# A convolution stage whose next tile is read out and gated between the last taps of the tile before it, with a ring of eight diagonals

## The chip, the cores and the metric

The kernel runs on one core of a Trainium2 chip. The metric is the device time of one execution in microseconds (us). Three executions of the kernel before took 2856.85, 2852.44 and 2855.83 us, median 2855.83. The engines are PE (TensorE; PEld is its weight load), DVE (VectorE), ACT (ScalarE), POOL (GpSimd) and SP (SyncE, which issues DMAs). Each works through its own instructions in the order in which they are written, and they meet only at semaphores.

## The reference

The kernel computes three blocks of a network with all its mixers and a mixture of experts. The change touches one stage of it, the convolution module of the second block, with D = 1024 channels and 512 tokens:

```python
CONV_C = 31
def causal_dwconv(x, w, b):           # one filter of 31 taps for each channel
    y = lax.conv_general_dilated(x, w[:, None, :], window_strides=(1,), padding=[(K - 1, 0)],
        dimension_numbers=("NWC", "WIO", "NWC"), feature_group_count=C)
    return y + b

def conformer_conv(x, norm, w1, b1, dw_w, dw_b, ln_g, ln_b, w2, b2):
    h = rms_norm(x, norm) @ w1 + b1   # 1024 -> 2048 channels
    h = jax.nn.glu(h, axis=-1)        # first half * sigmoid(second half)
    h = causal_dwconv(h, dw_w, dw_b)
    h = jax.nn.silu(layer_norm(h, ln_g, ln_b))
    return h @ w2 + b2
```

## The kernel before, in words

Channels lie on the 128 partitions and the 512 tokens along a row, so the stage has eight tiles j = 0 to 7 of 128 channels. Products in fp32 are made of three matmuls: each operand is split into a rounded high part and the remainder (hi·hi, hi·lo, lo·hi; `split_matmul`, line 526).

For tile j, in the words used below:

- **Projection** (PE, `pointwise` in `pe_conformer`): two banks, c1 (the value half) and c2 (the gate half), each 8 x 3 matmuls, 48 in all.
- **Read-out** (DVE, `pointwise` in `dve_conformer`): first the split of a unit of weights for a later tile (`w_lo`, line 513), then c2 times the norm's factor into `c_t2` (line 1560), then c1 into `c_t1` (line 1562).
- **Gating**: ACT takes the sigmoid of `c_t2` (line 1508), DVE makes `c_t1` = (c1 + bias) * sigmoid ("glu", line 1570, recorded at the helper's line 548).
- **Split of the gated tile**: ACT writes `c_t_hi` (line 1515), DVE the remainder `c_t_lo` (line 1580).
- **Taps on the vector side**: ACT starts `c_h` with the newest tap and the bias ("last tap", line 1511). DVE adds 17 more taps to it, one instruction each, each of which waits for the one before (lines 1573 to 1577, recorded at line 548; the width tells the tap: 495 columns is the first, 511 the last).
- **Taps on PE**: the 13 oldest taps are matmuls with a diagonal matrix of the tap's weights, 3 matmuls a tap, 39 a tile, into one bank. ACT makes each diagonal as two instructions, high and low (lines 1521, 1524), in a ring of 4 places: diagonal n waits until PE has used diagonal n - 4.
- **Joining** ("h", line 1587): DVE adds PE's bank to `c_h` when the tile's 13 diagonals are through.

PE runs one projection ahead: projection 0, projection 1, diagonals 0, projection 2, diagonals 1, and so on; at the end diagonals 6 and diagonals 7 follow one another. After them PE sums the eight tiles of `c_h` with a matrix of ones (16 matmul records), and the layer norm, which needs all eight tiles, begins with ACT's `c_mu` (line 1529). The orders on DVE and ACT are those of the Python loops; no scheduler changes them.

Of the kernel before, what the change touches and what calls it, by code (L numbers as in the profile page):

```python
# [8 lines left out]
F32 = mybir.dt.float32  # L9
# [7 lines left out]
P = 128  # L17
# [194 lines left out]
def build(nc, stream, vectors, consts, rconsts, x_in, mem_in, gates_w, group_w, lora_w,  # L212
# [95 lines left out]
    with ExitStack() as ph:  # L308
        c_s_hi, c_s_lo = sb(ph, "c_s_hi", [P, KT, S], F32R), sb(ph, "c_s_lo", [P, KT, S], F32R)
        c_h = sb(ph, "c_h", [P, KT, S])  # L310
        c_t1 = sb(ph, "c_t1", [P, 2, S])
        c_t2 = sb(ph, "c_t2", [P, 2, S])
        c_mu = sb(ph, "c_mu", [P, S])
        c_diag_hi, c_diag_lo = sb(ph, "c_diag_hi", [P, 4, P], F32R), sb(ph, "c_diag_lo", [P, 4, P], F32R)

        C_PAD = 16
        c_t_hi, c_t_lo = (sb(ph, f"c_t_{m}", [P, 2, C_PAD + S], F32R) for m in ("hi", "lo"))
        c_taps_hi, c_taps_lo = sb(ph, "c_taps_hi", [P, KT * CONV_C], F32R), sb(ph, "c_taps_lo", [P, KT * CONV_C])
# [209 lines left out]
    def split_matmul(T, out_ap, l_hi, l_lo, r_hi, r_lo, first, last):  # L528
        matmul(T, out_ap, l_hi, r_hi, first, False)
        matmul(T, out_ap, l_hi, r_lo, False, False)  # L530
        return matmul(T, out_ap, l_lo, r_hi, False, last)
# [925 lines left out]
    def pe_conformer(T):  # L1457
        n_diag = 0

        def pointwise(j):  # L1460
            n = place[("pw1", j)]
            b = take_bank(T, ("c1", j), dve_c, "t1", j)
            project(T, n, 2 * P, 0, ring1["xg"], range(KT), b, pe_c, ("c1", j), xg_ready(3) if j == 0 else None)
            b = take_bank(T, ("c2", j), dve_c, "t2", j)
            project(T, n, 2 * P, 1, ring1["xg"], range(KT), b, pe_c, ("c2", j))

        pointwise(0)
        for j in range(KT):
            i = j % 2
            if j + 1 < KT:  # L1470
                pointwise(j + 1)
            b = take_bank(T, ("conv", j), dve_c, "h", j)
            for m, k in enumerate(c_order):
                sh = CONV_C - 1 - k
                T.wait_ge(*act_c.at("diag", n_diag))
                if m == 0:
                    T.wait_ge(*dve_c.at("t_lo", j))
                odd = sh % 2
                moved = slice(C_PAD - odd, C_PAD + S - sh)
                split_matmul(T, b[:, sh - odd:], c_diag_hi[:, n_diag % 4, :], c_diag_lo[:, n_diag % 4, :],  # L1480
                             c_t_hi[:, i, moved], c_t_lo[:, i, moved], m == 0,
                             m == len(c_order) - 1).then_inc(*pe_c.mark("conv", n_diag))
                n_diag += 1
        b = take_bank(T, ("c_mean",), act_c, "mean")
        for j in range(KT):
            T.wait_ge(*dve_c.at("h", j))
            mm = matmul(T, b[:, :], const("ones"), c_h[:, j, :], j == 0, j == KT - 1)
        mm.then_inc(*pe_c.mark("mean"))
        b = take_bank(T, ("c_var",), act_c, "root")
        for j in range(KT):  # L1490
            T.wait_ge(*act_c.at("square", j))
            matmul(T, b[:, :], const("ones"), square[:, j % 2, :], j == 0, j == KT - 1).then_inc(*pe_c.mark("var", j))
        pe_out(T, units_of("pw2", 4), 2 * P, (c_s_hi, c_s_lo), range(KT), pe_c, ("x",), 4,
               ready=lambda k: dve_c.at("s_lo", k), after=lambda T: pe_xa_begin(T, 1))

    def act_conformer(A):
        n_diag = 0
        taps = slice(col["c_dw_w"], col["c_dw_w"] + KT * CONV_C)
        A.wait_ge(*normed(3))
        A.activation(c_taps_hi[:, :], vec[:, taps], ACT.Copy).then_inc(*act_c.mark("taps_hi"))  # L1500
        for part in (c_t_hi, c_t_lo):
            A.activation(part[:, :, 0:C_PAD], const("ident")[:, 0:2 * C_PAD].rearrange("p (i c) -> p i c", i=2),
                         ACT.Copy, scale=0.0).then_inc(*act_c.mark("zeros", part is c_t_lo))
        act_take(A, place[("pw1", 0)])
        for j in range(KT):
            i = j % 2
            A.wait_ge(*dve_c.at("t2", j))
            A.activation(c_t2[:, i, :], c_t2[:, i, :], ACT.Sigmoid, bias=vcol("c_b1", KT + j)).then_inc(
                *act_c.mark("sigmoid", j))
            A.wait_ge(*dve_c.at("glu", j))  # L1510
            A.activation(c_h[:, j, :], c_t1[:, i, :], ACT.Identity, scale=c_tap(j)(CONV_C - 1),  # L1511
                         bias=vcol("c_dw_b", j)).then_inc(*act_c.mark("last_tap", j))
            if j >= 2:
                A.wait_ge(*pe_c.at("conv", n_diag - len(c_order) - 1))
            A.activation(c_t_hi[:, i, C_PAD:], c_t1[:, i, :], ACT.Copy).then_inc(*act_c.mark("t_hi", j))
            if j + 1 < KT:
                act_take(A, place[("pw1", j + 1)])
            for k in c_order:
                if n_diag >= 4:
                    A.wait_ge(*pe_c.at("conv", n_diag - 4))  # L1520
                A.activation(c_diag_hi[:, n_diag % 4, :], const("ident"), ACT.Copy, scale=c_tap(j)(k)).then_inc(
                    *act_c.mark("diag_hi", n_diag))
                A.wait_ge(*dve_c.at("taps_lo"))
                A.activation(c_diag_lo[:, n_diag % 4, :], const("ident"), ACT.Copy,
                             scale=c_taps_lo[:, CONV_C * j + k:CONV_C * j + k + 1]).then_inc(
                    *act_c.mark("diag", n_diag))
                n_diag += 1
        A.wait_ge(*pe_c.at("mean"))
        A.activation(c_mu[:, :], held("c_mean")[:, :], ACT.Copy, scale=1.0 / D).then_inc(*act_c.mark("mean"))
        for j in range(KT):  # L1530
            A.wait_ge(*dve_c.at("centred", j))
            if j >= 2:
                A.wait_ge(*pe_c.at("var", j - 2))
            A.activation(square[:, j % 2, :], c_h[:, j, :], ACT.Square).then_inc(*act_c.mark("square", j))
        A.wait_ge(*pe_c.at("var", KT - 1))
        A.activation(c_mu[:, :], held("c_var")[:, :], ACT.Sqrt, scale=1.0 / D, bias=const("eps")).then_inc(
            *act_c.mark("root"))
        for j in range(KT):
            A.wait_ge(*dve_c.at("scaled", j))
            A.activation(c_h[:, j, :], c_h[:, j, :], ACT.Silu, bias=vcol("c_ln_b", j)).then_inc(*act_c.mark("silu", j))  # L1540
            A.wait_ge(*act_c.now())
            A.activation(c_s_hi[:, j, :], c_h[:, j, :], ACT.Copy).then_inc(*act_c.mark("s_hi", j))
        act_out(A, units_of("pw2", 4), 2 * P, dve_c, ("x",), 4, pe_c.at("c2", KT - 1), None,
                beside=lambda A, u: act_xa_mem(A, 1, u), after=lambda A: act_xa_begin(A, 1))

    def dve_conformer(V):
# [14 lines left out]
            V.wait_ge(*pe_c.at("c1", j))  # L1561
            V.tensor_tensor(c_t1[:, i, :], held("c1", j)[:, :], rstd[:, :], ALU.mult).then_inc(*dve_c.mark("t1", j))

        pointwise(0)
        for j in range(KT):
            i = j % 2
            V.wait_ge(*dve_c.at("t1", j))
            V.wait_ge(*act_c.at("sigmoid", j))
            V.wait_ge(*dve_c.now())
            stt(V, c_t1[:, i, :], c_t1[:, i, :], vcol("c_b1", j), c_t2[:, i, :], ALU.add, ALU.mult).then_inc(  # L1570
                *dve_c.mark("glu", j))
            V.wait_ge(*act_c.at("last_tap", j))
            for k in range(CONV_C_PE, CONV_C - 1):
                s = CONV_C - 1 - k
                V.wait_ge(*dve_c.now())
                stt(V, c_h[:, j, s:], c_t1[:, i, 0:S - s], c_tap(j)(k), c_h[:, j, s:], ALU.mult, ALU.add).then_inc(
                    *dve_c.mark("tap", j, k))
                if k == CONV_C_PE:
                    V.wait_ge(*act_c.at("t_hi", j))
                    V.tensor_tensor(c_t_lo[:, i, C_PAD:], c_t1[:, i, :], c_t_hi[:, i, C_PAD:].bitcast(F32),  # L1580
                                    ALU.subtract).then_inc(*dve_c.mark("t_lo", j))
            if j + 1 < KT:
                pointwise(j + 1)
            n_last += len(c_order)
            V.wait_ge(*pe_c.at("conv", n_last))
            V.wait_ge(*dve_c.now())
            V.tensor_tensor(c_h[:, j, c_base:], held("conv", j)[:, c_base:], c_h[:, j, c_base:], ALU.add).then_inc(
                *dve_c.mark("h", j))
# [1854 lines left out]
```

## Time and profile before

| | before |
|---|---|
| median of three executions | 2855.83 us |
| the profiled execution, its own time | 2851.64 us |
| its span in the trace | 2850.0 us |
| PE busy over the span | 2664.2 us (93%) |
| DVE busy over the span | 1828.0 us (64%) |
| ACT busy over the span | 1258.2 us (44%) |
| mean granted clock of PE, share of 2.4 GHz | 0.969 |
| the convolution stage, first gating to `c_mu` | 813.4 to 973.3 us |

Times in the trace count from the start of the span. "Busy" of PE is the time in which a matmul is under way; matmuls overlap (one of 512 columns lasts 0.39 us, but the next begins 0.22 to 0.23 us after it), so an engine that is 93% busy isn't 93% of its best. The stage in question takes 6% of the span, and all that comes later in the program stands behind it: its end sets when the rest begins.

### The profile page before, as it was taken

What the parts mean: (1) busy time and instruction counts of PE and PEld (TensorE: products, weight loads), DVE (VectorE), ACT (ScalarE), POOL (GpSimd) and SP (SyncE); (2) the same over time, 40 slices, a digit from 0 to 9 for tenths busy, and PEclk for the clock granted to TensorE, in tenths of its full rate; (3) what the DMA queues carried; (4) which work ended last, traced back from release to release, by engine and by line L of the source; (5) the groups of instructions that cost most, each with busy time, mean ns of one, the idle gap of its engine ahead of it and who ended that gap; (6) DMA issues with size and microseconds to landing.
All of it is one profiled execution on the core that took longest, in us unless ns stands there. A gap on an engine that the chain in (4) does not pass through costs nothing. (4 is left out here: it accounts for less than half of the span.)

```text
span 2850.0 us, 43296 instructions
## 1 busy us (share of the span) xinstructions
PE 2664.2 (93%) x18308; PEld 2160.3 (76%) x18308; DVE 1828.0 (64%) x2230; ACT 1258.2 (44%) x1676; POOL 272.2 (10%) x196
## 2 busy tenths in 40 slices
PE   8989999999999799999999999988888888799996
PEld 6767878888888588788888787766666666688885
DVE  7765456454579765464545676546758465799996
ACT  4453343232356553342323433443433233688884
POOL 1011010000000020100000200022112001132321
PEclk9999999999999999999999999998999999799998
DMA  4223222322221033223232353320000243899995
GB/s 166 80 89 113 98 89 89 104 98 94 91 71 46 33 115 106 87 89 104 89 103 89 114 189 108 148 67 20 23 20 13 73 138 119 320 384 375 379 375 224
DMA packets 87743, 365.81 MB, mean 128 GB/s; under 512 B 25472, under 2 KB 29568, under 8 KB 53888
## 3 DMA queue, kind: packets, MB, share of 16 engines
q1 hardware_dynamic: 77760, 338.40, 33.4%
q0 software_dynamic: 9792, 24.66, 2.5%
q8 instruction: 146, 2.39, 0.4%
q14 instruction: 45, 0.37, 0.0%
HBM read 346.23 MB, written 38.80 MB: 135 GB/s over the span
## 5 line engine op out<-in xcount | busy, mean ns | idle before, releaser
L526 PE MATMUL bank<-xg_hi,w_hi 128*128 128x512 f32 x1504 | 594.0, 395 | 12.0 <-DVE xg_lo L548 12.0
L526 PE MATMUL bank<-xg_hi,w_lo 128*128 128x512 f32 x1504 | 586.0, 390 | 0.0
L526 PE MATMUL bank<-xg_lo,w_hi 128*128 128x512 f32 x1504 | 585.9, 390 | 0.0
L513 DVE TENSOR_TENSOR w_lo<-w_raw,w_hi 128x2048 fp32r<-128x2048 f32 x165 | 378.9, 2297 | 197.4 <-ACT w_hi L509 197.3
L509 ACT ACTIVATE w_hi<-w_raw 128x2048 fp32r<-128x2048 f32 x165 | 314.3, 1906 | 231.2 <-PE bank L526 205.4
L526 PEld LDWEIGHTS bank<-xg_hi,w_hi 128*128 128x128 f32 x1504 | 282.7, 188 | 76.4 <-DVE w_lo L513 12.0
L526 PEld LDWEIGHTS bank<-xg_lo,w_hi 128*128 128x128 f32 x1504 | 282.7, 188 | 62.5 <-issue 4.3
L526 PEld LDWEIGHTS bank<-xg_hi,w_lo 128*128 128x128 f32 x1504 | 282.6, 188 | 58.8
L3140 DVE TENSOR_TENSOR w_lo<-e_w_raw,w_hi 128x2048 fp32r<-128x2048 f32 x77 | 174.5, 2286 | 10.6 <-ACT w_hi L2945 10.6
L2945 ACT ACTIVATE w_hi<-e_w_raw 128x2048 fp32r<-128x2048 f32 x77 | 147.7, 1918 | 29.4 <-PE bank L526 29.4
L526 PE MATMUL bank<-f_h_hi,w_hi 128*128 128x512 f32 x384 | 151.3, 394 | 0.0
L526 PE MATMUL bank<-f_h_hi,w_lo 128*128 128x512 f32 x384 | 150.5, 392 | 0.0
L526 PE MATMUL bank<-f_h_lo,w_hi 128*128 128x512 f32 x384 | 149.0, 388 | 0.0
L694 DVE TENSOR_TENSOR x<-bank,x 128x512 f32<-128x512 f32 x80 | 55.0, 688 | 122.7 <-PE bank L526 122.7
L526 PE MATMUL bank<-w_hi,e_h_hi 128*128 128x512 f32 x312 | 127.4, 408 | 5.1 <-DVE w_lo L3140 4.9
L526 PE MATMUL bank<-w_hi,e_h_lo 128*128 128x512 f32 x312 | 124.1, 398 | 0.0
L526 PE MATMUL bank<-w_lo,e_h_hi 128*128 128x512 f32 x312 | 123.8, 397 | 0.0
L548 DVE SCALAR_TENSOR_TENSOR c_h<-c_t,vec_sb,c_h 128x495 f32<-128x495 f32 (+16 forms) x136 | 101.1, 743 | 11.6 <-ACT c_h L1511 7.1
L1396 ACT ACTIVATE f_g<-f_z,vec_sb 128x512 f32<-128x512 f32 x48 | 39.2, 816 | 150.5 <-DVE f_z L1421 150.5
L548 DVE SCALAR_TENSOR_TENSOR f_g<-f_z,vec_sb,f_g 128x510 f32<-128x510 f32 x96 | 72.1, 751 | 44.2 <-ACT f_g L1396 42.5
L3140 DVE TENSOR_TENSOR w_lo<-w_raw,w_hi 128x2048 fp32r<-128x2048 f32 x40 | 91.4, 2287 | 7.2 <-ACT w_hi L2945 7.2
L587 ACT ACTIVATE xg_hi<-x,vec_sb 128x512 fp32r<-128x512 f32 x48 | 34.7, 724 | 122.7 <-DVE x L694 103.2
(498 smaller groups left out, 5336.1 us busy)
## 6 DMA issues: line engine op xcount, KB each, us to landing
w_raw<-stream SPq DMA_DIRECT2D x165, 1024.0 KB, 4.9
e_w_raw<-expert_rows SPq DMA_DIRECT2D x63, 1024.0 KB, 9.7
w_raw<-expert_rows SPq DMA_DIRECT2D x33, 1024.0 KB, 8.9
y_rows<-e_y_row SPq DMA_DIRECT2D x39, 512.0 KB, 8.9
p_spill<-p_stage SPq DMA_DIRECT2D x36, 256.0 KB, 2.3
mix_gate<-p_spill SPq DMA_DIRECT2D x16, 256.0 KB, 2.8
na_bias<-bias_na SPq DMA_DIRECT2D x16, 224.0 KB, 5.2
rw_rkv<-p_spill SPq DMA_DIRECT2D x12, 256.0 KB, 4.1
```

Of the source, the lines that this page charges most:

```text
L509: A.activation(ring(m)["hi"][m % SLOTS][:, :], ring(m)["raw"][m % RAW][:, :], ACT.Copy).then_inc(*w_hi.mark(m))
L513: V.tensor_tensor(ring(m)["lo"][m % SLOTS][:, :], ring(m)["raw"][m % RAW][:, :], ring(m)["hi"][m % SLOTS][:, :].bitcast(F32), ALU.subtract ...
L526: return T.matmul(out_ap, lhsT, rhs, start=first, stop=last, skip_group_check=True)
L548: return V.scalar_tensor_tensor(out=out_ap, in0=in0, scalar=scalar, in1=in1, op0=op0, op1=op1)
L587: A.activation(xg_of(i)[0][:, j, :], x[:, j, :], ACT.Identity, scale=vcol(NORMS[i], j)).then_inc(*act_norm.mark(i, "hi", j))
L694: V.tensor_tensor(x[:, j, :], held(*tag, j)[:, :], x[:, j, :], ALU.add).then_inc(*added.mark(*tag, j))
L1396: A.activation(m["g"][:, s, :], m["z"][:, s, :], ACT.Identity, scale=f_tap(l, ch)(CONV_F - 1), bias=vcol(f"f_dw_b{l}", ch)).then_inc(*act_ ...
L2945: A.activation(e_hi_of(n)[:, :], e_raws[n % RAWS], ACT.Copy).then_inc(*e_hi.mark(n))
L3140: V.tensor_tensor(e_lo_of(n)[:, :], e_raws[n % RAWS], e_hi_of(n)[:, :].bitcast(F32), ALU.subtract).then_inc(*e_lo.mark(n))
```

## The change

The ring of diagonals gets eight places. ACT's part for the next tile (sigmoid, `c_t_hi`, last tap) no longer follows a tile's diagonals: it stands before the ninth of the thirteen. Within that part `c_t_hi` now comes before the last tap. DVE reads out tile j + 1 after 14 of tile j's 17 taps, gates it before the last tap, and splits it before it joins tile j. PE's instructions and the DMAs keep their order.

```diff
-        c_diag_hi, c_diag_lo = sb(ph, "c_diag_hi", [P, 4, P], F32R), sb(ph, "c_diag_lo", [P, 4, P], F32R)
+        DIAGS = 8
+        c_diag_hi, c_diag_lo = (sb(ph, f"c_diag_{m}", [P, DIAGS, P], F32R) for m in ("hi", "lo"))
...
-        for j in range(KT):
+
+        def gated(j):
             i = j % 2
             A.wait_ge(*dve_c.at("t2", j))
             A.activation(c_t2[:, i, :], c_t2[:, i, :], ACT.Sigmoid, bias=vcol("c_b1", KT + j)).then_inc(
                 *act_c.mark("sigmoid", j))
             A.wait_ge(*dve_c.at("glu", j))
+            if j >= 2:
+                A.wait_ge(*pe_c.at("conv", (j - 1) * len(c_order) - 1))
+            A.activation(c_t_hi[:, i, C_PAD:], c_t1[:, i, :], ACT.Copy).then_inc(*act_c.mark("t_hi", j))
             A.activation(c_h[:, j, :], c_t1[:, i, :], ACT.Identity, scale=c_tap(j)(CONV_C - 1),
                          bias=vcol("c_dw_b", j)).then_inc(*act_c.mark("last_tap", j))
...
+        gated(0)
+        for j in range(KT):
             if j + 1 < KT:
                 act_take(A, place[("pw1", j + 1)])
-            for k in c_order:
-                if n_diag >= 4:
-                    A.wait_ge(*pe_c.at("conv", n_diag - 4))
...
+            for m, k in enumerate(c_order):
+                if m == DIAGS and j + 1 < KT:
+                    gated(j + 1)
+                if n_diag >= DIAGS:
+                    A.wait_ge(*pe_c.at("conv", n_diag - DIAGS))
...
+        pointwise(0)
+        gate(0)
+        low_part(0)
+        for j in range(KT):
+            i = j % 2
             V.wait_ge(*act_c.at("last_tap", j))
             for k in range(CONV_C_PE, CONV_C - 1):
-                s = CONV_C - 1 - k
+                left = CONV_C - 1 - k
+                if j + 1 < KT:
+                    if left == 3:
+                        pointwise(j + 1)
+                    if left == 1:
+                        gate(j + 1)
...
             if j + 1 < KT:
-                pointwise(j + 1)
+                low_part(j + 1)
             n_last += len(c_order)
             V.wait_ge(*pe_c.at("conv", n_last))
```

`gate(j)` is the glu, `low_part(j)` the instruction that writes `c_t_lo`; both are as before. ACT around the second tile's gating, before, from the thirteenth diagonal of tile 0 on (a name `c_t` stands for `c_t1` or `c_t2`; the brackets name the semaphores waited for):

```order
L1521 ACTIVATE c_diag_hi<-const_sb,vec_sb 128x128 [waits pe_conformer]
L1524 ACTIVATE c_diag_lo<-const_sb,c_taps_lo 128x128 [waits dve_conformer]
L1508 ACTIVATE c_t<-c_t,vec_sb 128x512 [waits dve_conformer]
L1511 ACTIVATE c_h<-c_t,vec_sb 128x512 [waits dve_conformer]
L1515 ACTIVATE c_t_hi<-c_t 128x512
L509 ACTIVATE w_hi<-w_raw 128x2048 [waits pe_conformer,w_raw0_load]
```

And now, from the eighth diagonal of tile 0 on; the last two rows are its ninth diagonal, and four more follow before the `w_hi`:

```order
L1528 ACTIVATE c_diag_hi<-const_sb,vec_sb 128x128
L1531 ACTIVATE c_diag_lo<-const_sb,c_taps_lo 128x128 [waits dve_conformer]
L1510 ACTIVATE c_t<-c_t,vec_sb 128x512 [waits dve_conformer]
L1515 ACTIVATE c_t_hi<-c_t 128x512 [waits dve_conformer]
L1516 ACTIVATE c_h<-c_t,vec_sb 128x512
L1528 ACTIVATE c_diag_hi<-const_sb,vec_sb 128x128 [waits pe_conformer]
L1531 ACTIVATE c_diag_lo<-const_sb,c_taps_lo 128x128 [waits dve_conformer]
```

What moved: the three instructions of the next tile, with their waits for DVE's `c_t2` and for its glu, stand ahead of the last five diagonals instead of behind them. DVE at the same place, before, from the last tap of tile 0 (511 columns) to the second tap of tile 1:

```order
L548 SCALAR_TENSOR_TENSOR c_h<-c_t,vec_sb,c_h 128x511 [waits dve_conformer]
L513 TENSOR_TENSOR w_lo<-w_raw,w_hi 128x2048 [waits w_hi_rounded]
L1560 TENSOR_TENSOR c_t<-bank,rstd 128x512 [waits pe_conformer]
L1562 TENSOR_TENSOR c_t<-bank,rstd 128x512 [waits pe_conformer]
L1587 TENSOR_TENSOR c_h<-bank,c_h 128x494 [waits dve_conformer,pe_conformer]
L548 SCALAR_TENSOR_TENSOR c_t<-c_t,vec_sb 128x512 [waits dve_conformer,act_conformer]
L548 SCALAR_TENSOR_TENSOR c_h<-c_t,vec_sb,c_h 128x495 [waits dve_conformer,act_conformer]
L1580 TENSOR_TENSOR c_t_lo<-c_t,c_t_hi 128x512 [waits act_conformer]
L548 SCALAR_TENSOR_TENSOR c_h<-c_t,vec_sb,c_h 128x496 [waits dve_conformer]
```

And now, from the fourteenth tap of tile 0 (508 columns) to the first of tile 1:

```order
L549 SCALAR_TENSOR_TENSOR c_h<-c_t,vec_sb,c_h 128x508 [waits dve_conformer]
L514 TENSOR_TENSOR w_lo<-w_raw,w_hi 128x2048 [waits w_hi_rounded]
L1567 TENSOR_TENSOR c_t<-bank,rstd 128x512 [waits pe_conformer]
L1569 TENSOR_TENSOR c_t<-bank,rstd 128x512 [waits pe_conformer]
L549 SCALAR_TENSOR_TENSOR c_h<-c_t,vec_sb,c_h 128x509 [waits dve_conformer]
L549 SCALAR_TENSOR_TENSOR c_h<-c_t,vec_sb,c_h 128x510 [waits dve_conformer]
L549 SCALAR_TENSOR_TENSOR c_t<-c_t,vec_sb 128x512 [waits dve_conformer,act_conformer]
L549 SCALAR_TENSOR_TENSOR c_h<-c_t,vec_sb,c_h 128x511 [waits dve_conformer]
L1581 TENSOR_TENSOR c_t_lo<-c_t,c_t_hi 128x512 [waits act_conformer]
L1606 TENSOR_TENSOR c_h<-bank,c_h 128x494 [waits dve_conformer,pe_conformer]
L549 SCALAR_TENSOR_TENSOR c_h<-c_t,vec_sb,c_h 128x495 [waits dve_conformer,act_conformer]
```

What moved: the read-out stands ahead of three taps, the glu ahead of one, and the join (`c_h<-bank`) now stands behind the glu and the split of the next tile, where it used to stand before both.

## Rows read from the trace of the kernel before

**Rows 1.** Busy time by engine in a stretch: PE, PEld, DVE, ACT, POOL, clock, DMA

```profile
845.00:865.00 20.00, 20.00 (x91) 16.79 (x90) 18.28 (x25) 12.74 (x32) 0.00 (x0) 1.00 0.16 53
```

**Rows 2.** Waits, 805 to 975 us: total us, times, longest

```profile
PEld bank L526 <- DVE c_t_lo L1580: 7.1, 1, 7.1
...
DVE c_h L548 <- ACT c_h L1511: 7.1, 8, 0.9
...
ACT c_diag_hi L1521 <- PE bank L526: 21.1, 11, 3.7
```

**Rows 3.** Timeline of PE: start us, us, instruction [idle before, releaser]

```profile
822.55 0.38 PE L526 MATMUL bank<-c_t_hi,c_diag_hi 128*128 128x494 f32 x1
...
831.19 0.39 PE L526 MATMUL bank<-xg_hi,w_hi 128*128 128x512 f32 x1
...
842.09 0.39 PE L526 MATMUL bank<-c_t_hi,c_diag_hi 128*128 128x494 f32 x1
...
948.03 0.38 PE L526 MATMUL bank<-c_t_hi,c_diag_lo 128*128 128x482 f32 x1
955.10 0.75 PE L526 MATMUL bank<-c_t_hi,c_diag_hi 128*128 128x494 f32 x1 [6.68 <-ACT c_diag_hi L1521]
...
960.51 0.39 PE L526 MATMUL bank<-c_t_lo,c_diag_hi 128*128 128x490 f32 x1
...
966.24 7.03 PE L526 MATMUL bank<-c_h,const_sb 128*128 128x512 f32 x16
```

**Rows 4.** Timeline of DVE: tile 0's glu, tiles 1 to 3, the end

```profile
813.41 0.75 DVE L548 SCALAR_TENSOR_TENSOR c_t<-c_t,vec_sb 128x512 f32<-128x512 f32 x1 [0.25 <-ACT c_t L1508]
...
852.44 0.67 DVE L1587 TENSOR_TENSOR c_h<-bank,c_h 128x494 f32<-128x494 f32 x1
853.25 0.75 DVE L548 SCALAR_TENSOR_TENSOR c_t<-c_t,vec_sb 128x512 f32<-128x512 f32 x1
...
855.53 0.68 DVE L1580 TENSOR_TENSOR c_t_lo<-c_t,c_t_hi 128x512 fp32r<-128x512 f32 x1
856.25 12.43 DVE L548 SCALAR_TENSOR_TENSOR c_h<-c_t,vec_sb,c_h 128x496 f32<-128x496 f32 x16
868.60 2.29 DVE L513 TENSOR_TENSOR w_lo<-w_raw,w_hi 128x2048 fp32r<-128x2048 f32 x1
870.80 0.68 DVE L1560 TENSOR_TENSOR c_t<-bank,rstd 128x512 f32<-128x512 f32 x1
...
872.19 0.67 DVE L1587 TENSOR_TENSOR c_h<-bank,c_h 128x494 f32<-128x494 f32 x1
...
954.26 0.69 DVE L1580 TENSOR_TENSOR c_t_lo<-c_t,c_t_hi 128x512 fp32r<-128x512 f32 x1
...
967.52 0.67 DVE L1587 TENSOR_TENSOR c_h<-bank,c_h 128x494 f32<-128x494 f32 x1
```

**Rows 5.** Timeline of ACT: tile 2's gating and first diagonal, and the end

```profile
854.04 0.81 ACT L1511 ACTIVATE c_h<-c_t,vec_sb 128x512 f32<-128x512 f32 x1 [1.53 <-DVE c_t L548]
854.76 0.62 ACT L1515 ACTIVATE c_t_hi<-c_t 128x512 fp32r<-128x512 f32 x1
855.28 1.91 ACT L509 ACTIVATE w_hi<-w_raw 128x2048 fp32r<-128x2048 f32 x1
857.08 0.39 ACT L1521 ACTIVATE c_diag_hi<-const_sb,vec_sb 128x128 fp32r<-128x128 f32 x1
857.37 0.40 ACT L1524 ACTIVATE c_diag_lo<-const_sb,c_taps_lo 128x128 fp32r<-128x128 f32 x1
...
973.31 0.60 ACT L1529 ACTIVATE c_mu<-bank 128x512 f32<-128x512 f32 x1 [8.81 <-PE bank L526]
```

**Rows 6.** Timeline of PE after other waits of 3 to 5 us, elsewhere in the program

```profile
185.80 0.79 PE L526 MATMUL bank<-ab_y_hi,w_hi 128*128 128x512 f32 x1 [3.02 <-DVE ab_y_lo L1042]
...
2311.41 0.50 PE L526 MATMUL bank<-mix_y_hi,w_hi 128*128 128x512 f32 x1 [4.58 <-DVE mix_y_lo L2380]
...
2312.29 0.63 PE L526 MATMUL bank<-mix_y_hi,w_hi 128*128 128x512 f32 x1
...
2315.27 0.51 PE L526 MATMUL bank<-mix_y_lo,w_hi 128*128 128x512 f32 x1
```

More of the change, by code:

```diff
@@ L1479, in pe_conformer @@
                 moved = slice(C_PAD - odd, C_PAD + S - sh)
-                split_matmul(T, b[:, sh - odd:], c_diag_hi[:, n_diag % 4, :], c_diag_lo[:, n_diag % 4, :],
+                split_matmul(T, b[:, sh - odd:], c_diag_hi[:, n_diag % DIAGS, :], c_diag_lo[:, n_diag % DIAGS, :],
                              c_t_hi[:, i, moved], c_t_lo[:, i, moved], m == 0,
@@ L1510, in act_conformer @@
             A.wait_ge(*dve_c.at("glu", j))
+            if j >= 2:
+                A.wait_ge(*pe_c.at("conv", (j - 1) * len(c_order) - 1))
+            A.activation(c_t_hi[:, i, C_PAD:], c_t1[:, i, :], ACT.Copy).then_inc(*act_c.mark("t_hi", j))
             A.activation(c_h[:, j, :], c_t1[:, i, :], ACT.Identity, scale=c_tap(j)(CONV_C - 1),
                          bias=vcol("c_dw_b", j)).then_inc(*act_c.mark("last_tap", j))
-            if j >= 2:
-                A.wait_ge(*pe_c.at("conv", n_diag - len(c_order) - 1))
-            A.activation(c_t_hi[:, i, C_PAD:], c_t1[:, i, :], ACT.Copy).then_inc(*act_c.mark("t_hi", j))
+        gated(0)
+        for j in range(KT):
             if j + 1 < KT:
                 act_take(A, place[("pw1", j + 1)])
-            for k in c_order:
-                if n_diag >= 4:
-                    A.wait_ge(*pe_c.at("conv", n_diag - 4))
-                A.activation(c_diag_hi[:, n_diag % 4, :], const("ident"), ACT.Copy, scale=c_tap(j)(k)).then_inc(
+            for m, k in enumerate(c_order):
[3 more added lines that the diff above has]
+                    A.wait_ge(*pe_c.at("conv", n_diag - DIAGS))
+                A.activation(c_diag_hi[:, n_diag % DIAGS, :], const("ident"), ACT.Copy, scale=c_tap(j)(k)).then_inc(
                     *act_c.mark("diag_hi", n_diag))
                 A.wait_ge(*dve_c.at("taps_lo"))
-                A.activation(c_diag_lo[:, n_diag % 4, :], const("ident"), ACT.Copy,
+                A.activation(c_diag_lo[:, n_diag % DIAGS, :], const("ident"), ACT.Copy,
                              scale=c_taps_lo[:, CONV_C * j + k:CONV_C * j + k + 1]).then_inc(
@@ L1562, in pointwise, with gate @@
             V.tensor_tensor(c_t1[:, i, :], held("c1", j)[:, :], rstd[:, :], ALU.mult).then_inc(*dve_c.mark("t1", j))
-        pointwise(0)
-        for j in range(KT):
+        def gate(j):
             i = j % 2
-            V.wait_ge(*dve_c.at("t1", j))
             V.wait_ge(*act_c.at("sigmoid", j))
@@ L1571, in dve_conformer, with low_part @@
                 *dve_c.mark("glu", j))
+        def low_part(j):
+            i = j % 2
+            V.wait_ge(*act_c.at("t_hi", j))
+            V.tensor_tensor(c_t_lo[:, i, C_PAD:], c_t1[:, i, :], c_t_hi[:, i, C_PAD:].bitcast(F32),
+                            ALU.subtract).then_inc(*dve_c.mark("t_lo", j))
+        pointwise(0)
+        gate(0)
+        low_part(0)
+        for j in range(KT):
+            i = j % 2
             V.wait_ge(*act_c.at("last_tap", j))
             for k in range(CONV_C_PE, CONV_C - 1):
-                s = CONV_C - 1 - k
-                V.wait_ge(*dve_c.now())
[L1576 to L1581, printed above, removed]
+                left = CONV_C - 1 - k
[4 more added lines that the diff above has]
+                        gate(j + 1)
+                V.wait_ge(*dve_c.now())
+                stt(V, c_h[:, j, left:], c_t1[:, i, 0:S - left], c_tap(j)(k), c_h[:, j, left:], ALU.mult,
+                    ALU.add).then_inc(*dve_c.mark("tap", j, k))
             if j + 1 < KT:
-                pointwise(j + 1)
+                low_part(j + 1)
             n_last += len(c_order)
```

## The prediction

> **What bounds the kernel now.** I read the busy time by stretch first, then the waits of the stage, then its timeline engine by engine. In the middle of the stage PE has no idle time and the full clock, 2.4 GHz (20.00 of 20 us, clock 1.00), while DVE is busy for 18.28 of 20 us [rows 1]. A tile costs PE 19.5 us: 39 diagonal matmuls from 822.55 to 831.19 (8.64 us, 0.2215 each) and 48 projection matmuls from 831.19 to 842.09 (10.90 us) [rows 3]. DVE needs 19.75 us a tile (852.44 to 872.19 [rows 4]), of which 0.88 us is a wait for ACT's last tap, 7.1 us over the eight tiles [rows 2]. So DVE falls back by about 0.2 us a tile, which nobody feels until the last one: PE, a projection ahead, meets only there a `c_t_lo` that isn't written. It stands for 6.68 us, and its next matmuls run at 1.2 GHz: 13 steps from 955.10 to 960.51 take 5.41 us, where 2.88 are due, 2.5 us lost [rows 3]. PE then goes on to the sums over the tiles (966.24, 7.03 us), and ACT's `c_mu` starts with their end at 973.31 [rows 3, 5]. DVE had joined the last tile at 968.19 [rows 4], while the sums of the other seven ran. So PE ends the stage, and what follows hangs on it.
>
> I write E(j) for the end of the last diagonal matmul of tile j. Before, E(0) is 831.35 (0.16 us after the start of its follower at 831.19, as the matmul lasts 0.38) and E(6) is 948.41 [rows 3].
>
> **What it removes.** Two things. The 0.88 us wait on DVE is covered: between glu and the next tile's first tap now stand one tap, the split and the join. And the 6.68 + 2.5 us of PE before the last tile's diagonals go, since `c_t_lo` of tile 7 is written before the join of tile 6. After E(6) PE would need 39 x 0.2215 − 0.16 = 8.48 us to the start of the sums, where it took 966.24 − 948.41 = 17.83: 9.35 less. What is late next there is DVE: from E(6) a join (0.85 to the first tap), 17 taps of 0.78 and about 0.1 (14.2 us), and the join of 0.67, 14.85 in all; the last of eight pairs of the sums would start at 8.48 + 14 x 0.43 = 14.5. So DVE gives 0.35 back: −9.0 us net.
>
> **What it adds.** ACT must pass sigmoid, `c_t_hi` and last tap of tile j+1 before it may write the ninth diagonal of tile j, and the second of these waits for DVE's glu(j+1). Queued behind are diagonals 9 to 13 of tile j; PE waits for them, and DVE's join of tile j waits for PE. The join in turn stands ahead of tile j+1's taps. This closes a circle, from E(j−1) to E(j), each step from rows of before:
>
> - E to the start of the join 0.04 (as from the sums' end, 973.27, to `c_mu`, 973.31), join to the next dependent instruction 0.81 (852.44 to 853.25): 0.85 [rows 3 to 5]
> - 14 taps: 16 taps took 12.35 us to the start of `w_lo`, that is 15 steps of 0.78 and a last of 0.65; so 13 x 0.78 + 0.65 = 10.8, to 11.65 [rows 4]
> - `w_lo` 2.20, read-out of both halves up to a dependent instruction 1.39 (870.80 to 872.19), two taps 1.56, glu 0.75: to 17.55 [rows 4]
> - hand-over to ACT 0.04, `c_t_hi` and last tap 1.24 (both together, 854.04 to 855.28), ninth diagonal, high and low, 0.69: to 19.5 [rows 4, 5]
> - hand-over to PE 0.15 (954.95 to 955.10): 19.65; then 15 matmuls, 14 x 0.2215 + 0.38 = 3.48 [rows 3, 4]
>
> The circle is 23.14 us long. PE itself is ready for the ninth diagonal after 10.90 + 24 x 0.2215 − 0.16 = 16.06 us, so it stands for about 3.6 us (3.4 by the ends of its matmuls) in each tile. The split of `w_hi` and the first eight diagonals are no limit: 1.8 us (855.28 to 857.08) and 16 x 0.29 us (857.08 to 857.37) of ACT, some 6.5 us [rows 5], within the projection's 10.90; the eight places allow them, since PE is through with the tile before. Read-out of c2 at 13.8 us comes after PE's projection at 10.8, so DVE doesn't wait for it. SP's loads keep their order and are released at the same step of the tile.
>
> Tile 0: glu ends at 814.16; `c_t_hi` (0.04 + 0.62), then hand-over and split up to the next tap (0.04 + 0.72, from 855.53 to 856.25) bring the first tap to 815.58. From there 23.14 − 0.85 = 22.29: E(0) = 837.87, 6.5 us later than before. PE stands for about 6.4 us [rows 4, 5].
>
> Six circles more: E(6) = 837.87 + 6 x 23.14 = 976.7 against 948.41, +28.3 us. With the −9.0 of the tail: **+19.3 us** at full clock.
>
> **The clock.** The trace of before has no wait of PE of 3.4 us that comes back every 23 us, so I bound it. Below by nothing. Above by the whole of the diagonals behind the wait at half the clock: 15 x 0.19 = 2.9 us a tile. Near it stand three rows: the wait of 6.68 us cost 2.5; after 3.02 us (and a short one just before) the next matmul lasts 0.79 us, 1.2 GHz from the start; after 4.58 us the clock held for three matmuls and then fell, seven steps in 2.98 us instead of 1.6, 1.4 us lost [rows 3, 6]. Tile 0's wait is like the first: +2.5. The other six I take at 1.4 us in half of the cases, 0.7 each: +4.2. All this lies on the circle, since DVE waits for the join. Sum: 19.3 + 2.5 + 4.2 = **+26.0 us**.
>
> The Trainium skill's page "TensorE: Matmul & The Clock Gate", section "HAM oscillation — how this bites in real kernels", says that a loop in which TensorE waits once per tile can lose the full clock anew in every tile. By it every one of the seven waits costs like the worst. The rows above bear it out for single waits, not for a row of them, and one of them kept the clock for a while.
>
> The profiled execution took 2851.64 us: 2877.6 for such a one. It is 4.2 us below the median of the runs, with which the result is compared, so I predict 2855.8 + 26.0 = **2882 us**.
>
> **Rivals.** What a measurement of this kernel can tell from no change is about 0.2%, 5.7 us.
>
> A. The circle at full clock but for tile 0: +21.8 us, or +19.3 without that too, 2875 to 2878. For it: the 4.58 us wait kept the clock for the first three matmuls. Against: the 3.02 us wait didn't.
>
> B. The clock falls in every tile, at 2.5 us each: 19.3 + 7 x 2.5 = +36.8, 2893; with 2.9 for the six it is 2895. The rule of the Trainium skill above would give this case.
>
> C. Only tile 0 stalls, because later tiles have slack that I don't see: E(0) is 6.5 + 2.5 = 9.0 late, the tail gives 9.0 back, 0 in sum, 2856. It needs the circle to be no longer than PE's own 19.5 us, 3.6 less than the rows say. I find no row that could be that much too long; DVE's chain alone has 17.5.
>
> D. Faster: the ScalarE part does no harm within the diagonals, and what remains is the tail. Its place is the ninth diagonal; it decides whether glu comes earlier than 14.1 us after E(j−1) (16.06 less 1.97 for ACT's part, the diagonal and PE's hand-over). Then PE keeps 19.5 a tile and the result is −9.0 us, 2847. The fourteen taps (10.8) with read-out and glu reach 17.55 by rows that hardly scatter, and tile 0 has no join ahead of it yet still comes at 832.4 against the 825.9 that PE's ninth diagonal allows (827.87 less 1.97). So this needs a wrong reading of the order.
>
> **Chances.** The circle with the clock lost in some tiles 0.57 (its own range 2878 to 2888), A 0.16, B 0.15, C 0.04, D 0.04, and a still larger loss from something the rows don't show (hand-overs that cost more, seven times over) 0.04. Faster 0.04; within 0.2% 0.04; slower 0.92. The range takes in A and B with some us for the scatter of the runs (2852 to 2857 before): 2869 to 2897.
>
> **What would show it.** PE in the stage: seven waits before the ninth diagonal, released by ACT's `c_diag`, the first near 6.4 us, the others near 3.4; diagonals of one tile every 23.1 us or a little more; 0.41 us steps behind some of them; no wait before tile 7's diagonals. DVE: a wait of some 4 us for PE before each join, none for the last tap. ACT: waits for glu before `c_t_hi`. `c_mu` near 1000 us instead of 973. It is wrong if PE has no wait at the ninth diagonal, or if the tile takes 20 us or less; the clock's share is wrong if the step after the waits is 0.22 us throughout.

## The result, and the profile after

| | before | after |
|---|---|---|
| median of five executions | 2855.83 us | 2887.31 us |
| range | 2852.44 to 2856.85 | 2885.69 to 2887.99 |
| the profiled execution, its own time | 2851.64 us | 2887.31 us |
| its span | 2850.0 us | 2885.7 us |
| stage: start of `rstd` ahead of it to start of `c_mu` | 171.5 us | 203.4 us |

The change makes the kernel slower: ratio 1.0115, 95% interval 1.0104 to 1.0125 (an estimate over all executions; the two medians alone give 1.0110, inside the interval). The forecast was 2882 us, slower. The stage alone grew by 31.8 us (`rstd` at 801.78 and `c_mu` at 973.31 before [rows 5], 802.88 and 1006.23 after), as much as the medians differ, 31.5. The rows of `rstd`, before and after, and of `c_mu` after:

```profile
801.78 3.35 DVE L647 RECIPROCAL rstd<-root 128x512 f32<-128x512 f32 x1 [1.70 <-ACT root L642]
```

```profile
802.88 3.35 DVE L648 RECIPROCAL rstd<-root 128x512 f32<-128x512 f32 x1 [1.70 <-ACT root L643]
```

```profile
1006.23 0.60 ACT L1536 ACTIVATE c_mu<-bank 128x512 f32<-128x512 f32 x1 [11.22 <-PE bank L527]
```

The profiled executions differ by 35.7 us: 1.1 arise ahead of the stage and 2.8 behind it. Of these 2.8, 1.5 come right behind `c_mu`, where PE waits 2.17 us for the squares of the layer norm. The sixteen matmuls after that wait took 7.67 us before, at full clock, and 9.18 after, with a mean granted clock of 0.74 in their first 2.9 us:

```profile
975.44 7.67 PE L526 MATMUL bank<-square,const_sb 128*128 128x512 f32 x16 [2.17 <-ACT square L1534]
```

```profile
1008.36 9.18 PE L527 MATMUL bank<-square,const_sb 128*128 128x512 f32 x16 [2.17 <-ACT square L1541]
```

The stretch from `c_mu` to the end took 1876.1 to 1878.8 us in the seven kernels below with a stage under 175 us, and 1879.5 to 1883.2 in the five with a longer one. Each of these is a single execution, and the clock behind `c_mu` doesn't explain it: e1_behind lost it too, e3_at_4 didn't. What the medians add to the difference of the stages, −1.6 us (e3_at_4) to +3.7 (e8_early_glu), follows no such order, and the cause stays open. To keep this part out, I compare stages.

The waits of the kernel after, all engines, 805 to 1005 us (who waited for whom: total us, times, longest):

```profile
ACT c_t L1510 <- DVE c_t L1567: 78.1, 8, 12.1
DVE c_h L1606 <- PE bank L527: 42.5, 7, 7.0
...
PE bank L527 <- ACT c_diag_lo L1531: 25.9, 7, 6.2
ACT c_t_hi L1515 <- DVE c_t L549: 16.9, 8, 2.3
...
DVE c_t_lo L1581 <- ACT c_t_hi L1515: 0.7, 1, 0.7
```

The rows show seven waits of PE for `c_diag`, seven of DVE's join for PE, and eight of ACT for DVE: three engines in a circle, each waiting for the next. Of [rows 2] two entries are gone: DVE's 7.1 us for the last tap, and PE's for `c_t_lo` before the last tile.

One turn of the circle, tile 2, on DVE:

```profile
865.00 0.67 DVE L1606 TENSOR_TENSOR c_h<-bank,c_h 128x494 f32<-128x494 f32 x1 [5.52 <-PE bank L527]
865.78 10.83 DVE L549 SCALAR_TENSOR_TENSOR c_h<-c_t,vec_sb,c_h 128x495 f32<-128x495 f32 x14
876.53 2.29 DVE L514 TENSOR_TENSOR w_lo<-w_raw,w_hi 128x2048 fp32r<-128x2048 f32 x1
878.73 0.69 DVE L1567 TENSOR_TENSOR c_t<-bank,rstd 128x512 f32<-128x512 f32 x1
...
881.69 0.75 DVE L549 SCALAR_TENSOR_TENSOR c_t<-c_t,vec_sb 128x512 f32<-128x512 f32 x1
...
890.71 0.67 DVE L1606 TENSOR_TENSOR c_h<-bank,c_h 128x494 f32<-128x494 f32 x1 [6.88 <-PE bank L527]
```

DVE does its 14 taps, the read-out and glu without a pause and then stands 6.88 us at the join. ACT one tile earlier, from the sigmoid to the ninth diagonal:

```profile
855.10 0.72 ACT L1510 ACTIVATE c_t<-c_t,vec_sb 128x512 f32<-128x512 f32 x1 [10.96 <-DVE c_t L1567]
858.12 0.63 ACT L1515 ACTIVATE c_t_hi<-c_t 128x512 fp32r<-128x512 f32 x1 [2.30 <-DVE c_t L549]
858.66 0.80 ACT L1516 ACTIVATE c_h<-c_t,vec_sb 128x512 f32<-128x512 f32 x1
859.37 0.39 ACT L1528 ACTIVATE c_diag_hi<-const_sb,vec_sb 128x128 fp32r<-128x128 f32 x1
859.66 0.39 ACT L1531 ACTIVATE c_diag_lo<-const_sb,c_taps_lo 128x128 fp32r<-128x128 f32 x1
```

And PE, the ninth diagonal of tile 1 and that of tile 2:

```profile
860.10 0.77 PE L527 MATMUL bank<-c_t_hi,c_diag_hi 128*128 128x486 f32 x1 [3.28 <-ACT c_diag_lo L1531]
860.67 0.61 PE L527 MATMUL bank<-c_t_lo,c_diag_hi 128*128 128x486 f32 x1
...
862.69 0.52 PE L527 MATMUL bank<-c_t_hi,c_diag_hi 128*128 128x484 f32 x1
863.05 0.38 PE L527 MATMUL bank<-c_t_lo,c_diag_hi 128*128 128x484 f32 x1
...
864.80 0.40 PE L527 MATMUL bank<-xg_hi,w_hi 128*128 128x512 f32 x1
...
884.45 0.77 PE L527 MATMUL bank<-c_t_hi,c_diag_hi 128*128 128x486 f32 x1 [3.26 <-ACT c_diag_lo L1531]
885.01 0.61 PE L527 MATMUL bank<-c_t_lo,c_diag_hi 128*128 128x486 f32 x1
```

The first wait ends at 860.10, 0.05 us after ACT's ninth diagonal does (859.66 + 0.39). A matmul of 486 columns that lasts 0.61 us and is followed after 0.41 runs at 1.2 GHz; at 2.4 GHz it lasts 0.38 and is followed after 0.22. In tile 1 the clock is back after about 3 us, in tile 2 it stays low through all fifteen matmuls. Where [rows 1] had PE busy for 20.00 of 20 us at clock 1.00, the same view now has

```profile
845.00:865.00 20.00, 16.72 (x69) 13.76 (x68) 13.95 (x19) 7.60 (x18) 0.00 (x0) 0.91 0.16 52
```

The end of the stage is as forecast: diagonals 7 follow diagonals 6 without a wait, and `c_mu` starts 16.0 us after E(6), the end of tile 6's diagonals (1006.23 − 990.23), where it took 24.9 before (973.31 − 948.41).

### The profile page after: what moved, and what is told of

Its sections match the earlier page's. It is cut to its first block and busy times, and to the rows that moved or that the text cites. A ratio compares the mean times of both kernels' runs of the same rounds, so it can differ in the third digit from the quotient of the medians.

```text
span 2885.7 us, 43302 instructions
## 1 busy us (share of the span) xinstructions
PE 2681.3 (93%) x18308; PEld 2171.4 (75%) x18308; DVE 1828.6 (63%) x2230; ACT 1252.3 (43%) x1676; POOL 271.9 (9%) x196
```

## The experiments

There are ten kernels. Those of one group of runs shared their executions of the kernel before. The numbers of all are from the profiled executions, the ratios from all executions. E(j) is the end of the last diagonal matmul of tile j, "tile" is (E(6) − E(0)) / 6, and "PE's wait" is the one in tiles 1 to 6:

| kernel | stage us | E(0) after `rstd` | tile us | E(6) to `c_mu` | PE's wait us | ratio to before (95%) |
|---|---|---|---|---|---|---|
| before | 171.5 | 29.6 | 19.51 | 24.9 | none | |
| after | 203.4 | 37.7 | 24.94 | 16.0 | 3.3 | 1.0115 (1.0104 to 1.0125) |
| e1_behind | 162.6 | 29.6 | 19.51 | 16.0 | none | 0.9971 (0.9961 to 0.9980) |
| e2_at_12 | 172.6 | 33.8 | 20.47 | 16.0 | 0.6, none in tile 1 | 1.0006 (0.9996 to 1.0015) |
| e3_at_4 | 222.8 | 41.5 | 27.54 | 16.0 | 5.9 | 1.0174 (1.0158 to 1.0189) |
| e4_filled | 190.4 | 36.1 | 23.06 | 16.0 | 0.8 | 1.0084 (1.0068 to 1.0099) |
| e5_ring8 | 171.8 | 29.6 | 19.51 | 25.1 | none | 0.9999 (0.9990 to 1.0008) |
| e6_sigmoid | 167.1 | 33.7 | 19.50 | 16.4 | none | 0.9984 (0.9975 to 0.9993) |
| e7_behind_ring4 | 163.9 | 29.6 | 19.51 | 17.3 | none | 0.9975 (0.9964 to 0.9985) |
| e8_early_glu | 170.1 | 34.3 | 19.98 | 16.0 | at most 0.5 | 1.0003 (0.9994 to 1.0012) |
| e9_at_10 | 187.5 | 36.3 | 22.50 | 16.2 | 1.4 to 2.0 | 1.0068 (1.0052 to 1.0085) |
| e10_at_9 | 195.5 | 37.7 | 23.64 | 16.0 | 2.2 in tile 1, then 2.6 | 1.0098 (1.0081 to 1.0115) |

### ScalarE's part behind the diagonals

```diff
             for m, k in enumerate(c_order):
-                if m == DIAGS and j + 1 < KT:
-                    gated(j + 1)
...
                 n_diag += 1
+            if j + 1 < KT:
+                gated(j + 1)
```

> The changed kernel, but ScalarE's sigmoid, c_t_hi and last tap of the next tile stand behind all 13 diagonals; ring of eight and DVE's new order stay. Theory (the circle glu -> ninth diagonal -> PE -> join -> taps is what costs): with no diagonal behind the wait for glu, the circle is open, PE keeps its 19.5 us a tile, has no wait in the stage, and the stage ends 9.0 us earlier than before: 2847 us, E(6) to E(0) 117 us. Rival 1 (DVE's new order costs by itself, glu and split ahead of the join): 2856 or more, with waits on DVE other than for PE. Rival 2 (the ring or its place in memory costs): about 2887 as in the changed kernel.

Measured: 2846.47 us (before 2856.07 in these runs). DVE in this kernel, one tile; in the tile shown there is no wait for the sigmoid, for `c_t_hi`, for the last tap or for PE:

```profile
870.86 0.67 DVE L1606 TENSOR_TENSOR c_h<-bank,c_h 128x494 f32<-128x494 f32 x1
871.64 10.83 DVE L549 SCALAR_TENSOR_TENSOR c_h<-c_t,vec_sb,c_h 128x495 f32<-128x495 f32 x14
...
887.55 0.75 DVE L549 SCALAR_TENSOR_TENSOR c_t<-c_t,vec_sb 128x512 f32<-128x512 f32 x1
888.33 0.75 DVE L549 SCALAR_TENSOR_TENSOR c_h<-c_t,vec_sb,c_h 128x511 f32<-128x511 f32 x1
889.00 0.69 DVE L1581 TENSOR_TENSOR c_t_lo<-c_t,c_t_hi 128x512 fp32r<-128x512 f32 x1
889.79 0.67 DVE L1606 TENSOR_TENSOR c_h<-bank,c_h 128x494 f32<-128x494 f32 x1
```

This tile takes DVE 18.93 us (19.75 before, [rows 4]), so DVE catches up with PE, and waits for it only at the joins of tiles 5 and 6 (0.6 and 0.7 us). PE has no wait from the first diagonals to the sums. The gain is all at the end of the stage, 8.9 us, as the forecast had worked out for its tail. So DVE's new order is good, and with that order the loss comes from ScalarE's place. The kernel is faster than both the one before and the one after, and with e7_behind_ring4, from which the runs don't set it apart, the fastest here. ScalarE's new place with DVE's old order was not run: by the orders written out above it couldn't finish, since there the glu that ScalarE waits for stands behind a join that needs the diagonals behind ScalarE's wait.

### Before the thirteenth, the eleventh, the tenth and the fifth diagonal

Each of these four changes one number, here that of the first:

```diff
-                if m == DIAGS and j + 1 < KT:
+                if m == 12 and j + 1 < KT:
```

> The changed kernel, but ScalarE's part for the next tile stands before the thirteenth diagonal instead of the ninth. Theory: the circle holds one diagonal behind the wait instead of five, 19.5 + 0.82 = 20.3 us a tile, PE waits 0.8 us a tile with the clock kept; tile 0 3.7 us late, six tiles 4.8 us, tail -9.0: 2855 to 2856 us. Rival (what costs is any pass through ScalarE's part within the diagonals, wherever it stands): 2880 or more.

> The changed kernel, but ScalarE's part stands before the fifth diagonal. Theory: nine diagonals lie behind the wait, circle 25.6 us a tile at full clock, PE waits 6 us a tile and loses the clock each time, 2.5 us: 28.1 us a tile, 2910 us; at full clock it would be 2892. Rival (place does not matter): 2887.

> The changed kernel, but ScalarE's part stands before the eleventh diagonal. Circle theory: three diagonals behind the wait, 21.6 us a tile, PE waits about 2.0 us a tile and 4.9 in tile 0. If waits of 2.0 us keep the clock (only tile 0's costs, 1.8): 5.0 late in tile 0, 12.8 over six tiles, tail -9.0, clock 1.8: +10.6, 2866 us on a before of 2855. If the clock falls behind 2.0 us waits as it does behind 3.3 us: steps of 0.41 us in every tile and up to 2876.

> The changed kernel, but ScalarE's part stands before the tenth diagonal. Circle theory: four diagonals behind the wait, 22.3 us a tile, PE waits about 2.6 us a tile and 5.5 in tile 0. With the clock kept but in tile 0: 5.7 + 16.8 - 9.0 + 1.8 = +15.3, 2870 us; with the clock lost in some tiles (a wait of 2.6 us cost six slow steps in another run, 1.1 us): up to +23, 2878.

Measured, in this order: 2856.27, 2905.72, 2872.78 and 2882.13 us. PE's steady wait grows with each diagonal that stands behind ScalarE's wait, because PE comes to it 0.66 us sooner, while the diagonal itself comes when glu lets it: 0.6, 2.0, 2.6, 3.3 (the changed kernel) and 5.9 us with 1, 3, 4, 5 and 9 behind it. The other side of this is the sharpest sign of the circle: from E(j − 1) to PE's restart in tile j it is 19.47 to 19.50 us in every tile with such a wait, in these four kernels, in the changed one and in the one with fillers below, wherever ScalarE's part stands. Two of the rows, PE at the thirteenth diagonal in e2_at_12 and at the fifth in e3_at_4:

```profile
896.98 0.49 PE L527 MATMUL bank<-c_t_hi,c_diag_hi 128*128 128x482 f32 x1 [0.63 <-ACT c_diag_lo L1531]
```

```profile
863.72 0.77 PE L527 MATMUL bank<-c_t_hi,c_diag_hi 128*128 128x490 f32 x1 [5.92 <-ACT c_diag_lo L1531]
```

e2 came out as the theory had it (2855 to 2856). e3 came out 4 us below its 2910: PE's wait is the forecast 6 us, but the low clock behind it cost 1.6 to 2.2 us a tile (its 27 matmuls took 7.85 to 8.49 us, where they would take 6.25 at full clock, an estimate from a first step of 0.33, steps of 0.2215 and a last of 0.38) instead of the 2.5 that I had taken. The rivals with one price for all places (2880 or more, and 2887) are out. e9 and e10 were slower than the full-clock figures (2866 and 2870): e9 lies between its two, e10 above even its upper one, 27.6 us above before where I had allowed 23. Two things make this up. The clock fell in five of the six tiles after the first, and the twelve matmuls took 4.4 us there instead of 2.9, so it cost 1.5 us each time and not 1.1. With tile 0 that gives a stage that is 24.0 us longer. The other 3.6 us of the medians lie outside the stage, and their cause stays open. What both kernels say of the clock is taken together below.

### Fillers in PE's wait

```diff
             for m, k in enumerate(c_order):
                 sh = CONV_C - 1 - k
+                if m == DIAGS and j + 1 < KT:
+                    for filler in range(22 if j == 0 else 11):
+                        matmul(T, bank[7][:, :], c_t_hi[:, i, C_PAD:C_PAD + P], c_t_hi[:, i, C_PAD:C_PAD + S], True, True)
                 T.wait_ge(*act_c.at("diag", n_diag))
```

> The changed kernel with filler matmuls on PE ahead of the ninth diagonal of tiles 0 to 6 (22 in tile 0, 11 in the others, 512 columns each, into a bank that nobody reads), so that PE does work while it waits for ScalarE. The circle is the same; only the clock can change. Theory (1.2 GHz behind each wait costs 2.0 us a tile, on the circle): the tiles come every 23.0 us instead of 24.9, no 0.41 us steps, 2887.3 - 13.5 = 2874 us. Rival (the slow steps do not come from PE's wait, or they lie beside the circle): 2887 or more.

Measured: 2878.29 us, and a stage 12.9 us shorter than in the changed kernel (expected 13.5). PE, tile 1:

```profile
854.24 2.67 PE L527 MATMUL bank<-c_t_hi 128*128 128x512 f32 x11
857.69 0.49 PE L527 MATMUL bank<-c_t_hi,c_diag_hi 128*128 128x486 f32 x1 [0.78 <-ACT c_diag_lo L1534]
858.02 0.38 PE L527 MATMUL bank<-c_t_lo,c_diag_hi 128*128 128x486 f32 x1
...
860.88 0.38 PE L527 MATMUL bank<-c_t_hi,c_diag_lo 128*128 128x482 f32 x1
```

No step of 0.41 us is left in the stage's tiles, and the fifteen matmuls take 857.69 to 861.26, 3.57 us, where the changed kernel took 4.86 (860.10 to 864.96) to 6.33. PE did more work and the kernel became faster than the changed one, though it is still slower than before. This is the circle alone, at full clock: 23.06 us a tile. The kernel's median fell by less than the stage (by 9.0 us); behind the stage the profiled execution took 1882.5 us against 1879.5, and the cause stays open.

### The ring alone

```diff
-        c_diag_hi, c_diag_lo = sb(ph, "c_diag_hi", [P, 4, P], F32R), sb(ph, "c_diag_lo", [P, 4, P], F32R)
+        DIAGS = 8
...
-                if n_diag >= 4:
-                    A.wait_ge(*pe_c.at("conv", n_diag - 4))
+                if n_diag >= DIAGS:
+                    A.wait_ge(*pe_c.at("conv", n_diag - DIAGS))
```

> The kernel before with nothing changed but the ring of diagonals: eight places instead of four. Theory: PE waits for a diagonal nowhere but in the last tile, where it is c_t_lo that comes last, so 2856 us, no change, and ScalarE only gets ahead earlier. Rival (the ring carries part of the gain that the kernel with ScalarE's part behind the diagonals showed, 9.6 us): 2847 to 2853 us.

Measured: 2854.56 us beside 2854.65, no change. ACT's wait for PE falls from 21.1 us [rows 2] to 3.4, and its wait for DVE's `c_t2` grows from 26.4 to 44.9, so ACT gets ahead and then waits for DVE instead. The wait before the last tile's diagonals stays at 6.7 us:

```profile
ACT c_t L1509 <- DVE c_t L1561: 44.9, 8, 6.6
...
DVE c_h L549 <- ACT c_h L1512: 7.1, 8, 0.9
...
PE bank L527 <- ACT c_diag_hi L1522: 6.7, 1, 6.7
ACT c_diag_hi L1522 <- PE bank L527: 3.4, 5, 1.4
```

### Only the sigmoid within

`gated(j + 1)`, ahead of the ninth diagonal, keeps only the sigmoid; the wait for glu, `c_t_hi` and the last tap become a function of their own:

```diff
+        def split(j):
+            i = j % 2
             A.wait_ge(*dve_c.at("glu", j))
...
         gated(0)
+        split(0)
...
                 n_diag += 1
+            if j + 1 < KT:
+                split(j + 1)
```

> The changed kernel, but only the sigmoid of the next tile stays ahead of the ninth diagonal; c_t_hi and the last tap, with the wait for glu, go behind the thirteenth. Theory (it is the wait for glu that closes the circle, not a pass through ScalarE's work): the ninth diagonal hangs on the read-out of c2 alone, 14.6 + 0.62 + 0.69 + 0.15 = 16.0 us after E(j-1), just when PE is ready; a wait of about 2 us in tile 0, next to none later, 19.5 us a tile: 2847 to 2849 us. Rival (any wait of ScalarE for DVE within the diagonals stalls PE): 2865 or more.

Measured: 2850.08 us, faster than before (0.9984, 0.9975 to 0.9993) and above the 2847 to 2849 expected. The theory holds: tiles come every 19.5 us, so a pass through ScalarE's work within the diagonals, and even a wait for DVE there, costs nothing as long as what is waited for comes in time. What I had too small is tile 0. I allowed it a wait of about 2 us and no clock, and it is 4.2 us late:

```profile
830.90 0.77 PE L527 MATMUL bank<-c_t_hi,c_diag_hi 128*128 128x486 f32 x1 [2.59 <-ACT c_diag_lo L1535]
831.47 0.61 PE L527 MATMUL bank<-c_t_lo,c_diag_hi 128*128 128x486 f32 x1
```

Its wait is 2.6 us, and the clock behind it cost another 1.3 (the fifteen matmuls took 4.87 us instead of 3.57).

### ScalarE's part behind the diagonals, with four places

The first experiment's edit, and

```diff
-        DIAGS = 8
+        DIAGS = 4
```

> ScalarE's part behind all diagonals, DVE's new order, and the old ring of four places. Theory (the gain is DVE's order; the ring only let the diagonals run ahead): the last diagonal now waits for PE's ninth, some 2.8 us before E(j), the sigmoid comes 1.4 us before E(j) and DVE waits there for up to 1 us, inside its slack; PE keeps 19.5 us a tile: 2847 us, as with eight. Rival (the ring of eight is needed): above 2850 us, with PE waiting before c_t_lo or the first diagonals.

Measured: 2846.94 us, a gain of the same size as with eight places in e1 (ratios 0.9975 and 0.9971, intervals that overlap). The ring of eight isn't needed for the gain; it only saves a wait of 1.54 us before the last tile's first diagonal:

```profile
950.66 0.47 PE L527 MATMUL bank<-c_t_hi,c_diag_hi 128*128 128x494 f32 x1 [1.54 <-ACT c_diag_lo L1529]
```

### Glu earlier on DVE

```diff
-                    if left == 3:
+                    if left == 6:
                         pointwise(j + 1)
-                    if left == 1:
+                    if left == 5:
                         gate(j + 1)
```

> The changed kernel with ScalarE's part still ahead of the ninth diagonal, but DVE reads out the next tile after 11 taps and gates it one tap later (after 14 and before the last in the changed kernel). Theory (only the distance from the join to glu counts): glu ends 14.4 us after E(j-1) instead of 17.4, PE waits about 0.4 us a tile, 19.9 us a tile, 3.3 us late in tile 0 and perhaps 2 more from the clock, tail -9.0: 2853 to 2855 us. Rival (within the diagonals ScalarE's part always costs several us a tile): 2870 or more.

Measured: 2856.94 us beside 2854.65, ratio 1.0003, so no difference, about 2 us above what was expected. Its stage is 1.4 us shorter than before's. The tiles come every 19.9 us (joins at 855.88 and 875.78; one later tile took 20.3), the forecast of the theory to the tenth:

```profile
855.88 0.67 DVE L1606 TENSOR_TENSOR c_h<-bank,c_h 128x494 f32<-128x494 f32 x1 [1.11 <-PE bank L527]
...
869.43 0.75 DVE L549 SCALAR_TENSOR_TENSOR c_t<-c_t,vec_sb 128x512 f32<-128x512 f32 x1
...
875.78 0.67 DVE L1606 TENSOR_TENSOR c_h<-bank,c_h 128x494 f32<-128x494 f32 x1 [1.08 <-PE bank L527]
```

ScalarE's part stands at the same place as in the changed kernel. Only glu comes 3.14 us sooner after the join (13.55 us instead of 16.69), and PE's restart comes sooner by as much: 16.35 us after E(j − 1) in five of the six tiles, instead of 19.49. Against the kernel before, the loss is gone, with the 8.9 us of the tail helping to pay for what is left. With the four places above this shows the circle from both of its sides.

## Why the prediction was right, and what it mis-sized

**The bound before: right.** The waits that the forecast named are the ones that went, and the kernel of the first experiment, which adds no wait for PE in their place, gains 8.9 us in the stage by it.

**The tail, −9.0 us: right.** 24.9 us became 16.0, that is −8.9. The last two sums began 14.83 us after E(6), where DVE's chain was worked out as 14.85.

**The circle, 23.14 us: right to 0.1.** At full clock it is 23.06 (fillers). From E(1) = 864.96 to PE's restart at 884.45 it took 19.49 us in the changed kernel; the forecast had 19.65. The fifteen matmuls took 3.57 instead of 3.48, since the first after a wait is followed after 0.33 us. So two errors of 0.16 and 0.09 partly cancel.

**Tile 0: right, its clock a little too dear.** PE restarted 32.5 us after `rstd` (835.37 − 802.88), as forecast (834.39 − 801.78 = 32.6). Then the low clock cost 1.7 us (840.61 − 835.37 = 5.24, less 3.57) instead of 2.5.

**The clock in the six other tiles: the term that was mis-sized.** I took 1.4 us in half of the cases, 0.7 a tile and 4.2 in all. Both halves of this were too small. The granted clock fell in every one of the six; the fifteen matmuls took 4.86, 6.23, 5.11, 5.04, 6.33 and 5.12 us, on average 5.45, which is 1.88 more than the 3.57 of the fillers' kernel, 11.3 in all. That is 7.1 us more than forecast. The terms then close: 26.0 + 7.1 − 0.8 (tile 0's clock) − 0.5 (six circles 0.08 shorter) + 0.1 (tail) − 0.1 (rounding) = 31.8 us, and the stage grew by 31.8. The forecast gave its highest chance, 0.57, to a clock that is lost in some of the tiles, at 2878 to 2888 us. The measured 2887.3 lies in that band, but not for that reason: the clock fell in every tile, at a price between the forecast's and B's. That the number fell there is in part luck. The row that decided the choice was the 4.58 us wait after which the clock held for three matmuls [rows 6]; the 3.02 us wait beside it, with the low clock from the first matmul on, was the nearer one in length, and I gave it half the weight.

**The rivals.** B (the clock falls in every tile, at 2.5 us each, 2893) had the frequency right and the price too high; the measured time lies between the forecast and B. The rule of the Trainium skill's page "TensorE: Matmul & The Clock Gate", section "HAM oscillation — how this bites in real kernels", held in its point for the changed kernel: a loop with a wait in each tile lost the clock in each tile. The runs also show loops with shorter waits in each tile, 0.6 us in e2_at_12, that kept it. A fell, and so did C (PE waited in all seven tiles) and D (2847 us is to be had, but with ScalarE's part behind the diagonals). Under D, two figures are off by 0.1 to 0.15 us: glu of tile 1 comes at 832.3 by its own terms and not at 832.4, and the 1.97 leaves out the hand-over of 0.15 us to PE. Neither changes the choice.

**The signs named beforehand** all showed: the first wait 6.2 us and the others 3.3 (forecast 6.4 and 3.4), none before tile 7's diagonals, DVE waiting at each join, none for the last tap. DVE's join waits were 5.5 to 7.0 us rather than "some 4", the difference being the clock on the circle. `c_mu` came at 1006 where I had said near 1000.

## What to carry to other kernels

When an instruction with a wait is put in the middle of a supply that another engine draws on, ask who waits for that engine, and whether the thing waited for stands behind it in a third engine's order. If so the waits form a circle, and its length, not any engine's load, sets the pace: add it up once round from the rows, compare it with the bounding engine's own time, and look at the place from which the difference starts. Here the place of three instructions, before or behind five diagonals, made the difference between 1.2% lost and 0.3% won. The circle also shrinks to nearly PE's own pace when what is waited for comes sooner, as the earlier glu showed. A stall on TensorE that repeats is to be priced together with the low clock behind it, whenever what follows the stall is on the circle.

## What the runs showed of the hardware that I had not expected

A short wait of PE can already bring the lower clock. In the stage PE ran densely before a wait and after it. After waits of 0.5, 0.6, 0.8, 1.25, 1.43, 1.54 and 1.55 us the matmuls kept 2.4 GHz. Of five waits of 1.8 to 2.2 us four lost it and one kept it: e9_at_10 lost it after 1.96 us, a few matmuls later,

```profile
857.31 0.48 PE L527 MATMUL bank<-c_t_hi,c_diag_hi 128*128 128x484 f32 x1 [1.96 <-ACT c_diag_lo L1531]
...
858.08 0.55 PE L527 MATMUL bank<-c_t_hi,c_diag_hi 128*128 128x484 f32 x1
858.43 0.61 PE L527 MATMUL bank<-c_t_lo,c_diag_hi 128*128 128x484 f32 x1
```

and e10_at_9 kept it after 2.20 us and lost it from the first matmul on after 2.60:

```profile
858.38 0.49 PE L527 MATMUL bank<-c_t_hi,c_diag_hi 128*128 128x486 f32 x1 [2.20 <-ACT c_diag_lo L1531]
858.71 0.38 PE L527 MATMUL bank<-c_t_lo,c_diag_hi 128*128 128x486 f32 x1
...
880.78 0.78 PE L527 MATMUL bank<-c_t_hi,c_diag_hi 128*128 128x486 f32 x1 [2.60 <-ACT c_diag_lo L1531]
881.36 0.61 PE L527 MATMUL bank<-c_t_lo,c_diag_hi 128*128 128x486 f32 x1
```

Every wait of 2.6 us or more in the stage, in all these kernels, was followed by steps of 0.4 us.

The length of the wait doesn't settle it alone. Right behind `c_mu` all twelve kernels have the same wait of 2.17 us, behind sums at full clock and ahead of the same sixteen matmuls. Six kept the clock (before, e2, e3, e5, e6, e7; 7.7 us), and six lost it for a while (after, e1, e4, e8, e9, e10; 9.2 to 9.4 us). The two rows in the section on the result are one of each.

Fillers kept the clock: some 2.5 us of them in a wait of 3.3 us (0.8 left idle), and twice as many in tile 0 (1.25 left idle), in all seven tiles. In the six tiles after the first they gained 1.9 us each.
